# A recurrence's chunk matrices: 128x128 products on block-diagonal tiles, or 64x64 blocks on quarters of the array

## The chip, the cores and the metric

The kernel runs on one core of a Trainium2 chip. The metric is the device time of one execution in microseconds, median of several runs. Engines: TensorE (PE in the profile, its weight loads PEld), VectorE (DVE), ScalarE (ACT), GpSimd (POOL, unused) and SyncE (SP), whose queue issues all DMAs.

## The reference, cut to what matters

Two transformer blocks in fp32 over 1024 tokens with 1024 channels. The first (latent attention, Fourier mixing, SwiGLU) is not touched. The second adds banded attention and a recurrence ("RWKV-7 time mix"), gates and merges them, and ends in a feed-forward part. The recurrence is over 8 heads of 64 channels; per token and head it updates a 64x64 state:

```
p = p + (prev - p) * shift_mu ; r, k, v, cw, ca, cg = split(p)
decay = exp(-exp(-softplus(-(w0 + tanh(cw) @ w2)) - 0.5)) ; a = sigmoid(a0 + ca @ a2) ; g = sigmoid(cg) @ g2
kk = normalised(k * k_k) ; k = k * (1 + (a - 1) * k_a)
step:  sa = state @ (-kk) ; state = state * decay + outer(sa, kk * a) + outer(v, k) ; y = state @ r
y = group_norm(y) * ln_w + ln_b + sum(r * k * r_k) * v ; y = y * g
```

The kernel does not step token by token. Within a chunk of 64 tokens it forms the matrices of the decayed products of a, b = kk * a, k and r with one another, inverts I minus the strictly triangular one, and gets from it, for each chunk, a 64x64 map of the state (MT), an addition (NN), a map to the output (R2) and an output from zero (Y0). Only "state = MT * state + NN" is serial over chunks.

## The kernel before, in words

Every engine runs one long program (class Program); engines meet by semaphores whose numbers come from a first, counting pass (`wait_ge` on a named event). A PSUM bank is claimed with `k.bank(group)`, which turns through the banks, and the claim waits for the reader of the last tenant.

The recurrence is in class Mixer. It is cut into 8 units j: head pair hp = j // 2 (two heads, one in partitions 0 to 63 and one in 64 to 127) and half th = j % 2 of the tokens (512 tokens, 8 chunks). While unit j's matrices are made, unit j+1 "enters" (its a, b, k, r are shifted, decayed and turned to rows) and unit j-1 "leaves" (eight serial state steps, the output product yt, group normalisation, gate). The three are Python generators on each engine; `together` takes one round of each in turn until all have ended, and that is the whole order of work:

```
together(*[self.chunk_tensor(e, j, s) for s in range(2)], *behind, *ahead)
```

So in each round the matrices of head s = 0 stand first, then those of s = 1, then the leaving unit's work, then the entering unit's. PE, ACT and DVE have such a line each (from L3386 on).

Matrices (`chunk_tensor`, `chunk_scalar`, `chunk_vector`, L3001 to L3238): a tile M of 128x(4x128) holds four pairs of chunks of one head; each 128x128 block is block-diagonal in its two 64-token chunks, cut so by a mask. The pair products ("a", "n", "ak", "arb", "ark") contract 64 channels of one head into 128x128. Fifteen kinds of 128x128 products follow in each strand s: squarings of the 16-block-diagonal part (a2, n2, a4, n4, a8), the inverse of that part (x2, x4, x8), and a substitution in four steps for the rest (y0, r1, y1, r2, y2, r3, y3). ACT copies the plain results out of PSUM (L3120), DVE masks (L3175) or adds (L3180). At the end r2m and y0m write R2 and Y0 into 64 partitions each, and mt0, nn0, mt1, nn1 are 64x64x64 products, four or eight in a row on one quarter of PE's array.

Entering (`enter_*`, L2831 to L2989): decay and rate (L199 from TH, WA), the sums over a head (from CN "bones"), four turns by PE (L2868) and their copies by ACT (L2874), and elementwise work on 128x512 halves H. ACT's function changes five times a unit, each with a table load (L2885, L2898, L2900, L3296, L3298). Leaving (`leave_*`, L3251 to L3338): state products and adds (L3316), yt, sums for mean and variance, Ln and Exp for the root, gate. Behind the stage, the last unit leaves beside the first products of class Gates.

Of the kernel before, what the change touches and what calls it, by code (L numbers as in the profile page):

```python
# [34 lines left out]
def shape_constants():  # L35
# [50 lines left out]
class Quiet:  # L86
# [7 lines left out]
    reciprocal = memset = tensor_tensor_scan = dma_start = skip  # L94
# [2590 lines left out]
class Mixer:  # L2685
# [9 lines left out]
    def __init__(self, k, into):  # L2695
# [24 lines left out]
        self.Rt, self.At, self.Bt, self.Kt, self.Atm, self.Btm, self.Ktm, self.Vtm = [tile(o) for o in (124, 128, 132, 136, 88, 92, 96, 100)]  # L2720
        self.GN = [half(148), half(150)]
        self.SCM = half(120)
        mats = [k.sb("M", [128, 4, 128], 156 + 2 * i) for i in range(24)]
        self.mats = [self.strand(mats[0:12]), self.strand(mats[12:24])]
# [6 lines left out]
    @staticmethod  # L2731
    def strand(m):

        A16, N16, R1, R2m, Ak, Arb, Ark, A2, N2, Xm, RHS, Rv = m
        return A16, N16, R1, R2m, Ak, Arb, Ark, A2, N2, Xm, RHS, N2, Rv, A2
# [43 lines left out]
    def shifted(self, e, n, mu, dst, a, b, event, last):  # L2779

        raw, k = self.RAW[n % 3], self.k
        e.wait_ge(("fetched", n))
        if a == 0:
            e.op.tensor_tensor(dst[:, 1:b], raw[:, 0:b - 1], raw[:, 1:b], ALU.subtract).then_inc(*e.event("mix_dve", ("step", *event)))
            e.op.tensor_scalar(dst[:, 0:1], raw[:, 0:1], -1.0, None, ALU.mult).then_inc(*e.event("mix_dve", ("step_0", *event)))
            e.wait_ge(("step_0", *event))
        else:
            e.op.tensor_tensor(dst[:, 0:b - a], raw[:, a - 1:b - 1], raw[:, a:b], ALU.subtract).then_inc(*e.event("mix_dve", ("step", *event)))
            e.wait_ge(("step", *event))
# [3 lines left out]
    def sums_tensor(self, e, group, src, *ready, lo=0, hi=8):  # L2793

        bank, free = self.k.bank(group, lo, hi)
# [3 lines left out]
    def begin_tensor(self, e, lo, hi):  # L2799
        yield  # L2800
        yield
        yield from self.enter_tensor(e, 0, lo, hi)
# [22 lines left out]
    def chunk(self, j, what):  # L2825

        return [("mm", ("chunk", j, s, what)) for s in range(2)] if j >= 0 else []

    def enter_tensor(self, e, j, lo=0, hi=8):  # L2831
        k, hp = self.k, j // 2
        r, k_, v, ld, a_, L, kk, E1, E2, Q1 = self.T
        for part, what in ((0, "decay"), (64, "rate")):
            group = (what, j)
            bank, free = k.bank(group, lo, hi)
            e.wait_ge(free, "w2", "a2", "tanh", ("shifted", "hidden"))
            mm(e, k.out(group), self.WA[part:part + 64, hp * 128:(hp + 1) * 128], self.TH[part:part + 64, self.columns_of(j)], True, True).then_inc(
                *e.event("mix_mm", ("mm", group)))
        yield  # L2840
        yield
        yield
        self.sums_tensor(e, ("squares", j), Q1[:, :], ("kk_square", j), lo=lo, hi=hi)
        for _ in range(5):
            yield
        self.sums_tensor(e, ("bonus", j), E2[:, :], ("rk", j), lo=lo, hi=hi)
        yield
        yield
        self.rows_tensor(e, j, "v_rows", v, ("shifted", "v", j), lo, hi)
        yield  # L2850
        yield
        yield
        self.rows_tensor(e, j, "a_rows", self.At[:, self.columns_of(j)], ("at", j), lo, hi)
        for _ in range(5):
            yield
        self.rows_tensor(e, j, "b_rows", a_, ("b_end", j), lo, hi)
        yield
        self.rows_tensor(e, j, "k_rows", k_, ("k_end", j), lo, hi)
        yield
        yield  # L2860

    def rows_tensor(self, e, j, what, src, ready, lo, hi):

        group = (what, j)
        bank, free = self.k.bank(group, lo, hi)
        e.wait_ge(free, ready)
        for i in range(4):
            x = e.op.transpose(self.k.out(group, 128, 128 * i), src[:, i * 128:(i + 1) * 128], self.k.cst("ident"))  # L2868
        x.then_inc(*e.event("mix_mm", ("mm", group)))

    def rows_copy(self, e, j, what, dst):

        e.wait_ge(("mm", (what, j)), *self.chunk(j - 2, "nn1"), *self.rhs_read(j - 2))
        e.op.activation(dst[:, self.columns_of(j)], self.k.out((what, j)), ACT.Copy).then_inc(*e.event("mix_act", ("read", (what, j))))  # L2874

    def rhs_read(self, j):
        return [("rhs", "chunk", j, s, "rhs") for s in range(2)] if j >= 0 else []

    def enter_scalar(self, e, j):
# [4 lines left out]
        e.wait_ge(("mm", ("decay", j)), ("at", j - 1) if j else None)  # L2884
# [3 lines left out]
        e.wait_ge(("read", ("decay", j)))  # L2888
        e.op.activation(ld[:, :], ld[:, :], ACT.Copy, scale=-float(np.exp(-0.5))).then_inc(*done("log_decay"))
# [5 lines left out]
        for _ in range(5):  # L2895
            yield
        e.wait_ge(("read", ("squares", j)))
        e.op.activation(E1[:, :], E1[:, :], ACT.Ln, scale=float(2.0 ** 30)).then_inc(*done("kk_log"))  # L2898
        e.wait_ge(("kk_log", j))
# [3 lines left out]
        e.op.activation(Q1[:, :], L[:, :], ACT.Exp).then_inc(*done("decay_in"))  # L2903
        yield
        e.wait_ge(("log_before", j))
        e.op.activation(ld[:, :], ld[:, :], ACT.Exp).then_inc(*done("decay_before"))
# [4 lines left out]
        e.wait_ge(("mm", ("bonus", j)), ("read", ("bonus", j)))  # L2911
        e.op.activation(E2[:, :], L[:, :], ACT.Exp, scale=-1.0).then_inc(*done("decay_out"))
        yield
        e.wait_ge(("log_end", j))
        e.op.activation(E1[:, :], E1[:, :], ACT.Exp).then_inc(*done("decay_end"))
        yield
        self.rows_copy(e, j, "a_rows", self.Atm)
        for _ in range(5):
            yield
# [5 lines left out]
    def enter_vector(self, e, j):  # L2925
        k, hp, sl = self.k, j // 2, self.columns_of(j)
# [3 lines left out]
        a, b, last = sl.start, sl.stop, j % 2 == 1  # L2930
        e.wait_ge(("mm", ("k_rows", j - 1)) if j else None)
        self.shifted(e, 2 + 3 * hp, 4 + hp, k_, a, b, ("k", j), last)
        yield
        self.shifted(e, 3 + 3 * hp, hp, r, a, b, ("r", j), last)
        yield
        e.wait_ge(("mm", ("v_rows", j - 1)) if j else None)
        self.shifted(e, 4 + 3 * hp, 8 + hp, v, a, b, ("v", j), last)
# [4 lines left out]
        e.wait_ge(("rate_k", j), ("kk", j), ("shifted", "k", j))  # L2942
        e.op.scalar_tensor_tensor(k_[:, :], E2[:, :], 1.0, k_[:, :], ALU.add, ALU.mult).then_inc(*done("key"))
        yield
        e.wait_ge("scan", ("log_decay", j))
        e.op.tensor_tensor_scan(L[:, :], self.SCM[:, :], ld[:, :], 0.0, ALU.mult, ALU.add).then_inc(*done("sum_log"))
# [3 lines left out]
        yield  # L2950
        e.wait_ge(("key", j), ("shifted", "r", j))
        e.op.scalar_tensor_tensor(E2[:, :], r[:, :], k.vec("r_k", hp), k_[:, :], ALU.mult, ALU.mult).then_inc(*done("rk"))
        yield
        e.wait_ge(("sum_log", j))
        e.op.tensor_tensor(ld[:, :], L[:, :], ld[:, :], ALU.subtract).then_inc(*done("log_before"))
        yield
        e.wait_ge(("kk_rnorm", j))
        e.op.tensor_tensor(kk[:, :], kk[:, :], E1[:, :], ALU.mult).then_inc(*done("kk_unit"))
        yield
        e.wait_ge(("mm", ("bonus", j)), ("shifted", "v", j))  # L2960
        e.op.tensor_tensor(BV, k.out(("bonus", j)), v[:, :], ALU.mult).then_inc(*e.event("mix_dve", ("read", ("bonus", j))))
        yield
        L3 = L[:, :].rearrange("p (c s) -> p c s", s=64)
        E3 = E1[:, :].rearrange("p (c s) -> p c s", s=64)
        e.wait_ge(("kk_unit", j))
        e.op.tensor_tensor(E3, L3[:, :, 63:64].broadcast_to([128, 8, 64]), L3, ALU.subtract).then_inc(*done("log_end"))
        yield
        e.wait_ge(("decay_before", j), ("kk_unit", j), *self.chunk(j - 2, "ark"))
        e.op.scalar_tensor_tensor(self.At[:, sl], kk[:, :], -1.0, ld[:, :], ALU.mult, ALU.mult).then_inc(*done("at"))
        yield  # L2970
        e.wait_ge(("decay_in", j))
        e.op.tensor_copy(self.GC[:, a // 64:b // 64], Q1[:, 63:512:64]).then_inc(*done("gc"))
        e.op.tensor_tensor(self.Rt[:, sl], r[:, :], Q1[:, :], ALU.mult).then_inc(*done("rt"))
        yield
# [4 lines left out]
        yield  # L2979
        e.op.tensor_tensor(self.Kt[:, sl], k_[:, :], E2[:, :], ALU.mult).then_inc(*done("kt"))  # L2980
        yield
        e.wait_ge(("decay_end", j))
        e.op.tensor_tensor(a_[:, :], a_[:, :], E1[:, :], ALU.mult).then_inc(*done("b_end"))
        yield
        e.op.tensor_tensor(k_[:, :], k_[:, :], E1[:, :], ALU.mult).then_inc(*done("k_end"))
        yield
# [800 lines left out]
```

## Time and profile before

| | us |
|---|---|
| timed runs, median (3 runs, 3459.4 to 3460.91) | 3460.9 |
| the profiled execution's own time, as its page gives it: the span | 3467.7 |
| PE busy in the span | 3300.9 (95%) |
| DVE busy | 2089.3 (60%) |
| ACT busy | 1468.8 (42%) |
| recurrence, first to last matrix product | 2034 to 2571 |

"Busy" is the union of an engine's instructions. Matmuls overlap, so a group's mean duration is longer than the step from one to the next. The granted clock is a share of 2.4 GHz: 0.50 is 1.2 GHz. An fp32 matmul stands in the trace as two records (a transposing one as one).

### The profile page before, as it was taken

To read this page: it belongs to the slowest core of one execution; us is meant where nothing else is said; L and a number is where in the kernel's file an instruction comes from. 1 tells how busy PE (TensorE), PEld (TensorE's weight loads), DVE (VectorE), ACT (ScalarE), POOL (GpSimd) and SP (SyncE) were. 2 spreads that over 40 slices of the span, in tenths; PEclk is the share of its full clock that TensorE was granted. 3 is DMA by queue.
4 is the path that set the end of the run, shared out by engine and by line. 5 is a ranking of instruction groups with operands and counts; after the bars stand their busy time and mean duration, and the time that the engine had idled before them with its cause. 6 is when DMAs were issued, how large, how long until landed. Compare 5 with 4: busy or idle time off the path is not lost.

```text
span 3467.7 us, 42391 instructions
## 1 busy us (share of the span) xinstructions
PE 3300.9 (95%) x16430; PEld 2572.9 (74%) x16430; DVE 2089.3 (60%) x3506; ACT 1468.8 (42%) x2635; POOL 0.2 (0%) x4
## 2 busy tenths in 40 slices
PE   8989999999999999999999998898999999999888
PEld 7456666788888877788886677787874788777766
DVE  3535766567666567755555766655544466655665
ACT  2213555553333345533335544444421464554333
POOL 0000000000000000000000000000000000000000
PEclk9999999999999999999997999999999999999999
DMA  6510000232333465433333000000022524455645
GB/s 258 182 43 1 1 1 13 73 104 82 94 114 105 149 215 177 151 110 103 116 100 134 16 19 7 13 26 1 1 82 89 187 95 136 143 175 188 207 159 181
DMA packets 254505, 351.21 MB, mean 101 GB/s; under 512 B 12385, under 2 KB 142049, under 8 KB 251105
## 3 DMA queue, kind: packets, MB, share of 16 engines
q1 hardware_dynamic: 254304, 348.50, 29.9%
q8 instruction: 131, 2.15, 0.3%
q14 instruction: 70, 0.57, 0.1%
HBM read 264.04 MB, written 84.41 MB: 100 GB/s over the span
## 4 chain that ended last, share of the span: by engine, by line
PE 74%; DVE 11%; DMA 8%; issue 3%; ACT 3%; SPq 0%; DVEq 0%; ACTq 0%
PE ps L199 72%; DMA wr<-in_w_down 6%; DVE wl L407 2%; DVE M L3175 1%; DMA hid<-ob 1%; PE ps L1573 1%; DVE NM L2430 1%; PE ps L935 1%; ACT wh L383 1%; DVE Yf L508 0%; DVE ob L1326 0%; DVE QT L2449 0%; DVE RT L2448 0%; DVE QT L2451 0%; PE ps L2868 0%
## 5 line engine op out<-in xcount | busy, mean ns | idle before, releaser
L199 PE MATMUL ps<-ffn_h,wh 128*128 128x512 f32 x2176 | 673.1, 390 | 9.8 <-DVE ob L1326 6.5
L407 DVE TENSOR_TENSOR wl<-wr,wh 128x512 fp32r<-128x512 f32 x610 | 403.1, 687 | 278.4 <-ACT wh L383 275.7
L383 ACT ACTIVATE wh<-wr 128x512 fp32r<-128x512 f32 x610 | 364.5, 625 | 457.3 <-PE ps L199 265.0
L199 PEld LDWEIGHTS ps<-ffn_h,wh 128*128 128x128 f32 x2176 | 408.2, 188 | 99.8 <-DVE ob L1326 10.8
L199 PE MATMUL ps<-ffn_h,wl 128*128 128x512 f32 x1088 | 424.1, 390 | 0.0
L199 PE MATMUL ps<-in_h,wh 128*128 128x512 f32 x1200 | 371.0, 390 | 4.5 <-DVE Yf L837 4.5
L199 PE MATMUL ps<-wh,wh 128*128 128x512 f32 x756 | 302.0, 399 | 40.4 <-DVE wl L407 40.0
L199 PE MATMUL ps<-M,M 128*128 128x128 f32 (+1 forms) x2176 | 293.7, 295 | 37.4 <-DVE ybT L3337 16.6
L199 PEld LDWEIGHTS ps<-M,M 128*128 128x128 f32 (+1 forms) x2176 | 274.5, 200 | 57.1 <-DVE ybT L3337 18.0
L199 PE MATMUL ps<-wl,wh 128*128 128x512 f32 x756 | 299.6, 396 | 0.0
L199 PE MATMUL ps<-wh,wl 128*128 128x512 f32 x756 | 299.3, 396 | 0.0
L199 PEld LDWEIGHTS ps<-in_h,wh 128*128 128x128 f32 x1200 | 225.9, 188 | 52.2 <-DVE Yf L837 4.9
L199 PEld LDWEIGHTS ps<-ffn_h,wl 128*128 128x128 f32 x1088 | 204.5, 188 | 42.4
L199 PE MATMUL ps<-in_h,wl 128*128 128x512 f32 x600 | 234.2, 390 | 0.0
L199 PEld LDWEIGHTS ps<-wh,wh 128*128 128x128 f32 x756 | 145.2, 192 | 80.7 <-DVE wl L407 51.0
L3120 ACT ACTIVATE M<-ps 128x512 f32<-128x512 f32 x144 | 85.0, 596 | 208.6 <-PE ps L199 208.6
L199 PEld LDWEIGHTS ps<-wh,wl 128*128 128x128 f32 x756 | 145.2, 192 | 31.0
L199 PEld LDWEIGHTS ps<-wl,wh 128*128 128x128 f32 x756 | 145.0, 192 | 29.8
L407 DVE TENSOR_TENSOR wl<-s,wh 128x512 fp32r<-128x512 f32 x100 | 68.9, 689 | 121.0 <-ACT wh L383 121.0
L383 ACT ACTIVATE wh<-T 128x512 fp32r<-128x512 f32 x108 | 65.7, 629 | 153.8 <-DVE T L415 110.1
L199 PEld LDWEIGHTS ps<-in_h,wl 128*128 128x128 f32 x600 | 112.9, 188 | 23.5
L2326 ACT ACTIVATE E<-ps 128x512 f32<-128x512 f32 x160 | 95.0, 594 | 69.5 <-PE ps L199 66.4
(360 smaller groups left out, 5375.5 us busy)
## 6 DMA issues: line engine op xcount, KB each, us to landing
hid<-ob SPq DMA_DIRECT2D x174, 256.0 KB, 2.3
wr<-hid SPq DMA_DIRECT2D x84, 512.0 KB, 4.4
wr<-in_w_down SPq DMA_DIRECT2D x72, 512.0 KB, 3.6
wr<-in_w_up SPq DMA_DIRECT2D x54, 512.0 KB, 4.5
wr<-in_w_in SPq DMA_DIRECT2D x42, 512.0 KB, 5.2
kept<-ob SPq DMA_DIRECT2D x84, 256.0 KB, 2.0
late<-in_w_ada SPq DMA_DIRECT2D x16, 1024.0 KB, 7.4
wr<-in_w_out SPq DMA_DIRECT2D x32, 512.0 KB, 4.3
```

The lines of the kernel that those rows point to most:

```text
L199: return e.op.matmul(out, left, right, start=start, stop=stop, skip_group_check=True)
L383: e.op.activation(self.rows(s)[0], src, ACT.Copy).then_inc(*e.event(self.name + "_act", ("w_high", self.name, s)))
L407: e.op.tensor_tensor(lo, src, hi.bitcast(F32), ALU.subtract).then_inc(*e.event(self.name + "_dve", ("w_low", self.name, s), *done))
L935: x = e.op.transpose(k.out(group, 128, 128 * j), self.XN[:, t, c * 128:(c + 1) * 128], k.cst("ident"))
L1573: x = e.op.transpose(self.k.ps[:, self.turn_bank(i, c) * 512 + j * 128:self.turn_bank(i, c) * 512 + (j + 1) * 128], self.P[i % 2][:, (c + ...
L2326: e.op.activation(x, self.bank(n % 3), ACT.Exp).then_inc(*e.event("att_exp", ("exp", n)))
L2430: e.op.tensor_reduce(self.NM[:, h % 2, t, i:i + 1], self.bank(self.MAX + self.chunks.index(chunk) % 2, b - a), AX.X, ALU.max, negate=True) ...
L3120: e.op.activation(dst[:, :, :], self.four(name(what)), ACT.Copy).then_inc(*e.event("chunk_act", ("read", name(what))))
L3175: x = e.op.tensor_tensor(dst[:, :, :], self.four(name(what)), bc(m), ALU.mult)
```

## The change

Every block of a chunk becomes a 64x64 matrix, stored with the two chunks of a pair in the two partition halves (M is now 128x(4x64)); products run on quarters of the array, the two chunks (c) on the two diagonal quarters in turn, or, where head and chunk both choose the quarter, on all four in turn. Masks are 64 wide. "n" and "arb" share a product (nr, 128 columns: Bt with At and Rt side by side), "ak" and "ark" too (kr). The inverse's last part is changed: gt = Aoff' X and g = X' Aoff, g2 = g squared, and two additions y1, y2 in place of the four-step substitution. Both heads are in one generator, one after the other in each round, and 20 rounds stand for some 28. Banks are fixed. Some entering work goes: the exponents "log_before" and "log_end" with their Exp on ACT, and the scaling of the log decay; a and r share a tile AR, b_end and k_end are made from Bt and Kt. The order within a round is turned round.

```
-            together(*[self.chunk_tensor(e, j, s) for s in range(2)], *behind, *ahead)
+            together(*behind, *ahead, self.chunk_tensor(e, j))
...
+    BANK = {"a": 0, "nr": 2, "kr": 4, "a2": 2, "n2": 0, "a4": 2, "xn4": 0, "x4": 4, "a8": 2, "akv": 0, "x8": 4, "gt": 2, "g": 0, "y0": 4,
+            "g2": 2, "y1": 0, "y2": 4, "out": 2, "state": 4}
...
+        four_ways = [(u, s, c) for u in range(4) for s, c in ((0, 0), (1, 1), (0, 1), (1, 0))]
...
+        def pairs(what, left, right, n):
+            for s in range(2):
+                claim(s, what)
+            for u, s, c in four_ways:
+                x = mm(e, k.out(name(s, what), n, n * u, part(c)), left(s, u, c), right(s, u, c), True, True)
...
+        def prod(what, left, right, n, *ready):
+            for s in range(2):
+                claim(s, what, *[(r, name(s, r[1])) if isinstance(r, str) else (r[0], name(s, r[1])) for r in ready])
+                for u in range(4):
+                    for c in range(2):
+                        x = mm(e, k.out(name(s, what), n, n * u, part(c)), left(s)[part(c), u, :], right(s)[part(c), u, :], True, True)
+                done(x, s, what)
...
+        pairs("a", at, bt, 64)
+        pairs("nr", bt, ar, 128)
+        pairs("kr", kt, ar, 128)
+        prod("a2", of(N16), of(A), 64, ("a16", "a"), ("read", "nr"))
+        prod("n2", of(A), of(N16), 64)
+        prod("a4", of(N2), of(A2), 64, ("read", "n2"), ("read", "a2"))
+        prod("xn4", of(A2), of(XN), 128, ("x1", "nr"))
+        prod("x4", of(A), of(X), 64, ("read", "a4"), ("x2", "xn4"))
+        prod("a8", of(N4), of(A), 64, ("read", "xn4"))
+        prod("akv", of(Ak), of(values), 64, ("read", "kr"))
+        prod("x8", of(A2), of(X), 64, ("read", "a8"), ("read", "x4"))
+        prod("gt", of(Aoff), of(X), 64, ("read", "x8"), ("read", "a"))
+        prod("g", of(X), of(Aoff), 64)
+        prod("y0", of(X), of(AV), 128, ("read", "akv"))
+        prod("g2", of(G), of(GT), 64, ("read", "g"), ("read", "gt"))
+        prod("y1", of(GT), of(WU), 128, ("read", "y0"))
+        prod("y2", of(A2), of(WU), 128, ("read", "g2"), ("read", "y1"))
```

Each `pairs` or `prod` call of that list is a round of its own (a yield stands behind each, and an empty round ahead of gt), counted from 0; "out" and "state" are rounds 18 and 19, with 48 products of 64x64x64 each that visit the four quarters in turn. In `enter_*` all groups but the rate use bank 6:

```
-        self.rows_tensor(e, j, "a_rows", self.At[:, self.columns_of(j)], ("at", j), lo, hi)
+        self.rows_tensor(e, j, "a_rows", lambda i: self.AR[:, 0, c + 2 * i:c + 2 * i + 2, :].rearrange("p a n -> p (a n)"), ("at", j))
...
+        _, free = self.k.settle(group, 6)
...
-        e.op.activation(ld[:, :], ld[:, :], ACT.Copy, scale=-float(np.exp(-0.5))).then_inc(*done("log_decay"))
...
-        e.op.activation(ld[:, :], ld[:, :], ACT.Exp).then_inc(*done("decay_before"))
-        e.op.activation(E1[:, :], E1[:, :], ACT.Exp).then_inc(*done("decay_end"))
+        e.op.activation(E2[:, :], L[:, :], ACT.Exp, scale=self.RATE).then_inc(*done("decay_out"))
```

Rounds of note: on PE squares 5, bonus 10, v_rows 13, a_rows 15; the state steps 2 to 9 (two empty rounds are put ahead of them), yt 10, mean 11, var 13, gate 16, all in bank 7. On ACT, Ln and Exp of the entering unit 8 and 9, of the leaving one both in 14, the copy of v_rows in 14, behind them the copies of y0. On DVE the scan with the key in 8. The first gate products turn through banks 0 to 6.

## Rows read from the trace of the kernel before

**Rows 1.** Table by stretch: length, busy us (instructions) per engine, clock, DMA share, GB/s.
```profile
2034.00:2571.00 537.00, 482.43 (x4470) 435.57 (x4468) 322.28 (x594) 227.71 (x359) 0.00 (x0) 0.94 0.03 11
```

**Rows 2.** Chain of waits over 2034 to 2571, shares by line.
```profile
by line: PE ps L199 68.5%; DVE M L3175 9.1%; issue 2.3%; ACT L3296 1.7%; ACT L3298 1.7%; DVE H L2790 1.5%; ACT M L3120 1.4%; PE ps L2868 1.3%; DVE M L3180 1.1%; DVE ybT L3337 0.9%; ACT H L3296 0.9%; ACT H L3298 0.8%; DVE H L2788 0.8%; DVE H
```

**Rows 3.** PE's waits there: total us, times, longest.
```profile
PE ps L199 <- DVE ybT L3337: 16.6, 7, 2.6
PE ps L199 <- DVE STt L3316: 14.3, 17, 1.5
```

**Rows 4.** PE in time (start, us, instruction): gate products, first and last state steps.
```profile
2088.55 0.33 PE L199 MATMUL ps<-STt,F 64*64 64x64 f32 x4
...
2126.41 1.02 PE L199 MATMUL ps<-SG,WG 128*128 128x512 f32 x2
...
2480.74 1.02 PE L199 MATMUL ps<-SG,WG 128*128 128x512 f32 x2
...
2514.08 0.33 PE L199 MATMUL ps<-STt,F 64*64 64x64 f32 x4
...
2572.08 0.33 PE L199 MATMUL ps<-STt,F 64*64 64x64 f32 x4 [0.67 <-ACT F L3162]
```

**Rows 5.** PE in time: starts of runs of products of each form.
```profile
2052.16 1.95 PE L199 MATMUL ps<-M,M 128*128 128x128 f32 x16
2054.04 1.71 PE L199 MATMUL ps<-F,F 64*128 64x128 f32 x16
2055.68 0.66 PE L2868 MATMUL ps<-CN,H 128*128 128x128 f32 x4
...
2112.28 1.15 PE L199 MATMUL ps<-F,STt 64*64 64x64 f32 x32
2113.35 1.12 PE L199 MATMUL ps<-H,CN 128*128 128x512 f32 x2
...
2293.42 0.27 PE L199 MATMUL ps<-M,F 128*64 128x128 f32 x1
...
2296.41 0.79 PE L199 MATMUL ps<-F,M 64*64 64x64 f32 x13
...
2302.54 0.33 PE L199 MATMUL ps<-STt,F 64*64 64x64 f32 x4
```

**Rows 6.** Groups of PE instructions in 2034 to 2571: the largest.
```profile
L199 PE MATMUL ps<-M,M 128*128 128x128 f32 x1920 | 261.6, 297 | 37.4 <-DVE ybT L3337 16.6 <-DVE H L2949 12.3 <-ACT M L3120 6.8
```

**Rows 7.** Groups of ACT and DVE instructions in the same stretch: busy us, mean ns.
```profile
L3120 ACT ACTIVATE M<-ps 128x512 f32<-128x512 f32 x144 | 85.0, 596 | 208.6 <-PE ps L199 208.6
L3162 ACT ACTIVATE F<-ps 64x256 f32<-64x256 f32 x31 | 11.7, 378 | 21.7 <-PE ps L199 21.7
L3298 ACT ACT_TABLE_LOAD x7 | 9.0, 1283 | 0.1
L3296 ACT ACTIVATE H<-ps,CN 128x512 f32<-128x512 f32 x7 | 4.8, 689 | 0.1
L3298 ACT ACTIVATE H<-H 128x512 f32<-128x512 f32 x7 | 4.4, 631 | 0.1
...
L3180 DVE TENSOR_TENSOR M<-ps,M 128x512 f32<-128x512 f32 x96 | 66.2, 691 | 96.6 <-PE ps L199 96.0
L3234 DVE TENSOR_TENSOR F<-F,ps 64x256 f32<-64x256 f32 x32 | 13.4, 419 | 21.1 <-PE ps L199 19.5
```

**Rows 8.** Clock: short stretches (columns as rows 1), PE after a wait, the page's strip.
```profile
2106.00:2110.00 4.00, 4.00 (x21) 3.66 (x21) 1.09 (x2) 2.40 (x3) 0.00 (x0) 0.50 0.00 0
1870.00:1885.00 15.00, 15.00 (x44) 9.23 (x44) 7.85 (x16) 5.91 (x12) 0.00 (x0) 0.50 0.01 2
2082.00:2086.00 4.00, 4.00 (x86) 3.83 (x86) 2.43 (x6) 1.35 (x3) 0.00 (x0) 1.00 0.02 4
...
2105.78 3.78 PE L199 MATMUL ps<-M,M 128*128 128x128 f32 x16 [1.92 <-DVE H L2949]
...
PEclk9999999999999999999997999999999999999999
```

More of the change, by code:

```diff
@@ L3107, in halves @@
[L3107 to L3127 removed]
+        e.wait_ge(("bt", j), ("gc", j))
@@ new lines, in chunk_scalar, with keep @@
+    def chunk_scalar(self, e, j):
+        k, th = self.k, j % 2
+        A, Aoff, A2, N4, GT, G, NR, KR, XN, WU = zip(*self.mats)
+        name = lambda s, what: ("chunk", j, s, what)
+        def keep(what, dst, a=0, b=64, n=64, after=None):
+            for s in range(2):
+                e.wait_ge(("mm", name(s, what)), (after, name(s, what)) if after else None)
+                e.op.activation(dst(s), self.four(name(s, what), a, b, n), ACT.Copy).then_inc(*e.event("chunk_act", ("read", name(s, what))))
+        for _ in range(3):
+            yield
+        keep("a2", lambda s: A2[s][:, :, :])
+        yield
+        keep("n2", lambda s: XN[s][:, :, 64:128])
+        yield
+        keep("a4", lambda s: A[s][:, :, :])
+        yield
+        keep("xn4", lambda s: N4[s][:, :, :], 64, 128, 128, "x2")
+        yield
+        yield
+        keep("a8", lambda s: A2[s][:, :, :])
+        yield
+        keep("akv", lambda s: self.AV[:, 4 * th:4 * th + 4, s, 64:128])
@@ L3156, in chunk_scalar @@
-        e.op.activation(self.Y0[rows, c0:c0 + 512], k.out(name("y0m"), 512, 0, rows), ACT.Copy).then_inc(*e.event("chunk_act", ("read", name("y0m"))))
-        yield
-        for h in range(2):
-            yield
-            e.wait_ge(("mm", name(f"nn{h}")), *self.left(j - 2))
-            o = k.out(name(f"nn{h}"), 256, 0, rows).rearrange("p (u n) -> p u n", u=4)
-            e.op.activation(self.halves(self.NN, s, th, h), o, ACT.Copy).then_inc(*e.event("chunk_act", ("read", name(f"nn{h}"))))
-            yield
@@ L3253, in leave_tensor @@
         Yt, yc = self.GN
-        made = [("read", ("chunk", j, s, w)) for s in range(2) for w in ("nn1", "mt1", "r2m", "y0m")]
+        made = [("read", ("chunk", j, c, w)) for c in range(2) for w in ("out", "state")]
+        yield
+        yield
         for i in range(8):
@@ L3395, in scalar @@
             ahead = [self.enter_scalar(e, j + 1)] if j + 1 < self.UNITS else []
-            together(*[self.chunk_scalar(e, j, s) for s in range(2)], *behind, *ahead)
+            together(*behind, *ahead, self.chunk_scalar(e, j))
         e.mark(("end", "chunks", e.name))
@@ L3412, in vector @@
             ahead = [self.enter_vector(e, j + 1)] if j + 1 < self.UNITS else []
-            together(*[self.chunk_vector(e, j, s) for s in range(2)], *behind, *ahead)
+            together(*behind, *ahead, self.chunk_vector(e, j))
         e.mark(("end", "chunks", e.name))
```

562 lines of the change are left out of this document (259 added, 303 removed).

## The prediction, made before the changed kernel ran

> **What bounds the kernel now.** I read the page first, where TensorE (PE) stands far ahead of the other engines in busy time, so a gain must come out of PE's own stream or out of its waits. The table by stage then places the change: the recurrence lasts from 2034 to 2571 us, 537 us, with PE busy for 482.4 of them, DVE for 322.3 and ACT for 227.7, at a mean granted clock of 0.94 [rows 1]. The chain of waits over that stretch runs through PE for over two thirds [rows 2]. So the stage is bound by PE's queue, with 537.0 - 482.4 = 54.6 us in which PE waits, 6.8 us a unit over eight units; the list of waits names the two largest: for the departing unit's last product, and for the state's serial steps [rows 3]. ACT's and DVE's waits are for PE and cost nothing.
>
> A unit's length is read from its gate product, which comes once a unit: from 2126.41 to 2480.74 there are five periods, so 354.33 / 5 = 70.9 us. The first unit, with nothing departing, takes from about 2034 to 2088.6 (55 us), the last, with nothing entering, from 2514.1 to 2572.1 (58 us) [rows 4].
>
> **Each product of now.** The trace writes an fp32 product as two records, so 16 records are 8 products. What counts is start to start, not the mean duration, since matmuls overlap. From [rows 5]: eight 128x128 products 2054.04 - 2052.16 = 1.88 us, 0.235 each; eight with 64 rows 2055.68 - 2054.04 = 1.64, 0.205 each; the 24 products of r2m and y0m, alternating between two column halves, 2296.41 - 2293.42 = 2.99, so 0.0623 a record; the 48 quarter products of mt and nn, run four or more on one quarter before the next, 2302.54 - 2296.41 = 6.13, so 0.064 a record; and the departing unit's yt, 16 quarter products that alternate between the two diagonal quarters, 2113.35 - 2112.28 = 1.07, so 0.0334 a record. That last pair of numbers is the heart of the case: the same 64x64x64 product costs 0.128 us when its neighbour sits on the same quarter and 0.067 when it sits on the other diagonal one.
>
> **PE, what goes.** Per unit the two strands issue 120 full products (15 kinds x 4 x 2; the stage's 1920 records / 2 / 8 agree [rows 6]): 28.2 us; 40 pair products: 8.2; 8 of akv, full weights and half the columns, at most the full product's 0.235: 1.9; r2m and y0m 3.0; mt and nn 6.1. Sum 47.4 us.
>
> **PE, what comes.** Products on 64x64 blocks: "a" 16, ten products of width 64 (a2, n2, a4, x4, a8, akv, x8, gt, g, g2) 160, out 48, state 48: 272 of width 64. Width 128: nr, kr, xn4, y0, y1, y2: 96. The 160 have exactly yt's form and order: 0.0334. For "a", out and state, which visit all four quarters, nothing in the trace shows four at once: between 0.0167 (twice yt's overlap) and 0.064 (none); I take yt's row, the nearest. 544 records x 0.0334 = 18.2 us. Width 128 on quarters is not in the trace either: below, 0.0334 (if issue and not columns set yt's pace); above, 0.1025, the 64-row product's step with no overlap; I take 0.0623, the two-half row, which streams the same 128 columns in pairs. 192 x 0.0623 = 12.0. Sum 30.2 us, so PE loses 17.2 us of work a unit.
>
> Weighed against this stands a rule. The row shows yt's two quarters, which differ in array rows and write one PSUM bank at different partitions, running at 0.0334 [rows 5]. The Trainium skill, page "TensorEngine Tiling (Array Packing)", section "Gotcha 1: PSUM Pressure", says that different row tiles cannot access the same PSUM bank at the same time. By that rule alone the products on the diagonal (all but "a", nr, kr, out, state) would run one by one; by the row they overlap. The trace disagrees with it for width 64, so I follow the trace and keep the rule as a rival.
>
> **PE, what stays.** Decay and rate, two sums, four turns, eight states, yt, mean, var, gate: about 10.4 us a unit by like rows (the period's remainder after 47.4 of matrices, 6.8 of waits and 4.0 for the half clock, below, is 12.7 and holds it).
>
> **Waits.** In the new order each round issues departing, then entering, then matrix work, on every engine, and a matrix step is one round for both heads. A 256-element copy by ACT takes 0.378 us where the 512-element one took 0.596, and DVE's add 0.419 for 0.691 [rows 7]. ACT's chunk work falls from 18 + 2 copies of 0.59 and 4 of 0.378 (13.4 us) to 22 of 0.378 and 2 of 0.596 (9.5); three entering activations of about 0.6 go too. DVE's falls from about 25.5 us (28 operations of 0.69, the rest halves) to 18 x 0.42 + 8 x 0.69 = 13.1, and two entering subtractions of 0.68 go. With 227.7 / 8 = 28.5 and 322.3 / 8 = 40.3 us busy before [rows 1] ACT is left at 23, DVE at 27: neither can be the bound. What is late next is a queue: in round 14 ACT stands through the departing Ln and Exp, each with a table load of 1.283 [rows 7], and the copy of the entering values' turn before it copies y0: 1.28 + 0.69 + 1.28 + 0.63 + 0.60 = 4.5 us. Behind PE's y0 (32 x 0.0623 = 2.0 us) stands the turn of a_rows, which now shares bank 6 with v_rows and waits for that copy, and behind it g2 and everything of the matrices. With ACT 0.7 late from g, PE waits 4.5 + 0.7 - 2.0 = 3.2 us. Round 9 waits for the state add behind DVE's scan and key, and bonus behind rk: 1.8. Elsewhere the first head's reader (0.38 to 0.42) is covered by the second head's product (0.53). Together 5.0 a unit, estimated; bounds 0, and 13 if each of the 20 rounds adds 0.4 of unhidden handing over (a quarter-product group of 0.53 us is shorter than product, reader and two hand-overs together).
>
> **The clock.** After a wait PE runs at half: in 2106 to 2110 the granted clock is 0.50 (1.2 GHz), and 16 records take 3.78 us instead of 1.95 [rows 8, 5]. At 0.94 mean, 2 x 0.06 x 537 = 64 us of the stage stood at 1.2 GHz, costing half, 32 us or 4.0 a unit. Waits a unit shrink only from 6.8 to 5.0, so I keep 4.0 of loss.
>
> **Sum.** New period 30.2 + 10.4 + 5.0 + 4.0 = 49.6 us instead of 70.9: 21.3 x 6 units = 128. The first unit loses 17.2 (it had nothing departing to wait for), the last 17.2 and some 3 of rounds (20 instead of 28): 38 together. 166 us in all. The attention ahead gets the first entering unit in fewer rounds on two banks, hidden beside PE's full queue; the gate stage behind gets seven banks for eight: 0. The profiled execution has a span of 3467.7, 6.8 above the median of the runs (3460.9, 0.2%): 3467.7 - 166 = 3301.7 on its own scale, 3295 on that of the timed runs.
>
> **Rivals.**
> (1) More overlap: four quarters at once in "a", nr, kr, out, state halves 7.5 + 4.0 us, and shorter waits leave the clock at 2.4 GHz: 5.7 + 4.0 a unit, 78 in all: 3217. For it: DVE and ACT have room. Against: the half clock came after waits under 3 us, which remain. 0.12.
> (2) Rounds bind: handing over costs 13 and not 5 a unit, since a round now holds one matrix step and no other strand fills it: 8 x 8 = 64 more: 3359. For it: the single strand. 0.12.
> (3) The diagonal quarters do not overlap in one bank: 320 records go from 0.0334 to 0.064 and 128 from 0.0623 to 0.1025, 14.9 a unit, 119: 3414. Against it yt's row. 0.07. If no quarters overlap at all (the change does not do what it says), matrices take 544 x 0.064 + 192 x 0.1025 = 54.5 us, 7 more than now, and with the waits the period is 73.9: about 3485. 0.03.
> (4) The other side: the stage falls to 1.2 GHz and stays there. In 1870 to 1885, among the attention's small products, PE is busy all the time and the clock is 0.50 [rows 8]. If quarter products can't lift the clock once a wait has lowered it, PE's 40.6 us become 81.2, the period 86, 15 longer than now: 8 x 15 = 120 slower, 3580. It decides where 70.9 - 45.6 = 25.3 of the 40.6 us, 62% of PE's work, runs at half clock. Against it: six microseconds of quarter products (2082 to 2088) (four of them in the row) ran at 1.00 [rows 8], and each fall in the stage ended within some 7 us. 0.05.
> The Trainium skill, page "TensorE: Matmul & The Clock Gate", section "What's actually happening", makes throttled the default and says that activity releases it; the attention's stretch shows that a busy engine alone need not, the recurrence that it mostly does.
>
> **Chances and range.** The forecast has 0.61, own range 3255 to 3335 (waits 0 to 10). The attention's half-clock stretch can also end earlier or later with the entering work's new order: the page's clock strip has 0.7 to 0.8 in that slice of 86.7 us [rows 8], so 35 to 52 us at 1.2 GHz, which cost 17 to 26: as much faster, or about as much slower; this is inside the range. From (1) to (2) 0.85 is held, less tails: 3215 to 3380. Faster by over 0.2% (7 us, about what a measurement here can tell from no change): forecast, (1), (2), (3)'s first half, 0.92; within 0.2% 0.01 (the edge of (3)'s second half); slower 0.07.
>
> **What would show it.** Right: the gate product returns every 45 to 54 us; the 64-wide products stand at 0.03 us a record in alternating quarters, the 128-wide at 0.053 to 0.063; PE's largest wait is ahead of the a_rows turn, for ACT; DVE and ACT at some 27 and 23 us a unit. Wrong: 0.06 a record for the diagonal products (3); a granted clock near 0.5 through the stage (4); PE waits over 10 us a unit spread over all rounds (2).

## The result, and the profile after

| us | before | changed |
|---|---|---|
| timed, median | 3460.9 (3459.4 to 3463.49) | 3264.78 (3259.7 to 3271.17, 4 runs) |
| profiled span | 3467.7 | 3257.9 |
| PE busy | 3300.9 | 3078.1 |
| recurrence, first entering product to the first product of the gate stage behind it (yaT,PW) | 2033.8 to 2572.3 | 2020.2 to 2355.7 |

The changed kernel takes 0.943 of the time before (95% interval 0.9417 to 0.9447). Some executions of either kernel run 100 to 120 us longer at a lower mean clock; the comparisons leave them out.

The stage itself shrank by 203.0 us, it began 13.6 us earlier, and what follows it took 6.8 us more. Together that is 209.8, the difference of the two spans. In the table by stretch (columns as in [rows 1]), the changed stage, and 45 us in its middle:

```profile
2022.00:2352.00 330.00, 275.22 (x6415) 218.56 (x6411) 212.97 (x454) 176.90 (x335) 0.00 (x0) 0.97 0.06 19
2118.00:2163.00 45.00, 37.29 (x852) 28.90 (x846) 29.30 (x65) 24.67 (x46) 0.00 (x0) 0.96 0.04 14
```

Beside [rows 1] the stage is still PE's (83% busy), but PE idles as much as it did, 54.8 us against 54.6, in a stage 203 us shorter. The chain of waits over 2022 to 2352, by line, answers to [rows 2]; PE's share fell from 68.5 to 54%:

```profile
by line: PE ps L198 54.0%; issue 4.7%; PE ps L2868 4.4%; DVE MM L3187 3.8%; ACT L3303 2.7%; ACT L3305 2.7%; DVE MM L3180 2.7%; DVE H L2798 2.6%; DVE H L2963 2.4%; ACT F L2883 1.8%; DVE STt L3325 1.6%; DVE F L2976 1.5%; DVE H L3332 1.5%; ACT
```

PE's waits in it (total us, times, longest). The two of [rows 3] are gone or small, and a new one is largest, six times 3.2 us: the turn of a_rows (L2868) waits for ACT's copy of v_rows (L2883).

```profile
PE ps L2868 <- ACT F L2883: 19.0, 6, 3.2
PE ps L198 <- DVE MM L3187: 7.5, 9, 0.9
PE ps L198 <- ACT F L2883: 7.2, 6, 1.2
PE ps L198 <- DVE STt L3325: 5.9, 19, 0.5
PE ps L198 <- issue: 4.3, 8, 1.2
```

ScalarE's own rows at that wait show what stands ahead of the copy: Ln (L3303) and Exp (L3305) of the departing unit, each with its table load.

```profile
2080.98 1.28 ACT L3303 ACT_TABLE_LOAD   x1
...
2082.98 1.28 ACT L3305 ACT_TABLE_LOAD   x1
...
2084.81 0.58 ACT L2883 ACTIVATE F<-ps 128x512 f32<-128x512 f32 x1
```

PE in time, one unit from its first entering product (TH,WA) to the next's, and the last such product but one, which gives the period (start, us, instruction; the answer to [rows 4, 5]):

```profile
2056.39 1.13 PE L198 MATMUL ps<-TH,WA 64*128 64x512 f32 x4 [1.17 <-ACT F L2883]
2057.44 0.69 PE L198 MATMUL ps<-F,AR 64*64 64x64 f32 x32
2057.96 1.06 PE L198 MATMUL ps<-AR,F 64*64 64x128 f32 x32
2058.96 0.27 PE L198 MATMUL ps<-STt,F 64*64 64x64 f32 x2
...
2065.88 1.92 PE L198 MATMUL ps<-MM,M 64*64 64x128 f32 x32
2067.62 0.28 PE L198 MATMUL ps<-STt,F 64*64 64x64 f32 x4
...
2078.80 0.66 PE L2868 MATMUL ps<-CN,H 128*128 128x128 f32 x4
2079.38 1.15 PE L198 MATMUL ps<-M,MM 64*64 64x64 f32 x32
2080.37 1.92 PE L198 MATMUL ps<-AV,MM 64*64 64x128 f32 x32
2085.44 1.10 PE L2868 MATMUL ps<-CN,AR 128*128 128x128 f32 x4 [3.16 <-ACT F L2883]
2086.48 1.97 PE L198 MATMUL ps<-M,M 64*64 64x64 f32 x32
2088.38 1.37 PE L198 MATMUL ps<-SG,WG 128*128 128x512 f32 x2
2089.68 4.04 PE L198 MATMUL ps<-MM,M 64*64 64x128 f32 x64
2094.59 0.46 PE L198 MATMUL ps<-MM,MM 64*64 64x64 f32 x16 [0.88 <-DVE MM L3187]
...
2096.15 0.66 PE L2868 MATMUL ps<-CN,H 128*128 128x128 f32 x4
2096.74 0.34 PE L198 MATMUL ps<-F,MM 64*64 64x64 f32 x8
...
2098.68 0.66 PE L2868 MATMUL ps<-CN,H 128*128 128x128 f32 x4
2100.56 1.13 PE L198 MATMUL ps<-TH,WA 64*128 64x512 f32 x4 [1.22 <-ACT F L2883]
...
2278.14 1.13 PE L198 MATMUL ps<-TH,WA 64*128 64x512 f32 x4 [1.20 <-ACT F L2883]
```

Period: (2278.14 - 2056.39) / 5 = 44.35 us, forecast 49.6, before 70.9. Steps from start to start: "a" 2057.96 - 2057.44 = 0.52 us for 32 records in all four quarters, 0.0163 each; nr 1.00 for 32 of width 128, 0.031; a diagonal product of width 64 2080.37 - 2079.38 = 0.99, 0.031; of width 128 2067.62 - 2065.88 = 1.74, 0.054; out 2096.15 - 2094.59 = 1.56 for 96, 0.0163; state 2098.68 - 2096.74 = 1.94 for 96, 0.020. Behind the 3.16-us wait the turn takes 1.10 us where its like took 0.66, and M,M 1.97 where it took 1.15: half clock. The table by stretch agrees, before and behind the wait:

```profile
2060.00:2085.00 25.00, 20.39 (x430) 15.87 (x424) 19.49 (x47) 16.06 (x30) 0.00 (x0) 1.00 0.01 2
2085.30:2088.60 3.30, 3.16 (x37) 2.71 (x38) 0.93 (x2) 1.55 (x5) 0.00 (x0) 0.53 0.02 5
```

From the turn to the products behind the gate product it is 2089.68 - 2085.44 = 4.24 us; at full clock 0.58 + 0.98 + 1.02 = 2.6: 1.7 us lost, once a unit.

Groups of ACT and DVE in the stage (busy, mean ns), against [rows 7]: the readers have the sizes that the other shapes of before gave.

```profile
L3132 ACT ACTIVATE M<-ps 128x256 f32<-128x256 f32 x112 | 41.1, 381 | 67.8 <-PE ps L198 54.7 <-DVE MM L3187 10.8
L3187 DVE TENSOR_TENSOR MM<-ps,MM 128x256 f32<-128x256 f32 x48 | 19.2, 422 | 16.6 <-PE ps L198 16.5
```

### The profile page after: what moved, and what is told of

The parts are those of the page before. It is cut to its first block, busy times and chain, and to the rows that moved or that the text cites. A ratio compares the mean times of both kernels' runs of the same rounds, so it can differ in the third digit from the quotient of the medians.

```text
span 3257.9 us, 46321 instructions
## 1 busy us (share of the span) xinstructions
PE 3078.1 (94%) x18478; PEld 2345.0 (72%) x18478; DVE 1979.6 (61%) x3370; ACT 1417.1 (43%) x2611; POOL 0.2 (0%) x4
## 4 chain that ended last, share of the span: by engine, by line
PE 73%; DVE 11%; DMA 8%; issue 4%; ACT 3%; SPq 0%; DVEq 0%; ACTq 0%
PE ps L198 71%; DMA wr<-in_w_down 6%; DVE wl L406 3%; DMA hid<-ob 2%; PE ps L1572 1%; DVE NM L2429 1%; PE ps L934 1%; ACT wh L382 1%; PE ps L2868 0%; DMA wr<-hid 0%; DVE MM L3187 0%; DVE ob L1325 0%; DVE Yf L507 0%; DVE QT L2448 0%; DVE RT L2447 0%
## 5 line engine op out<-in xcount | busy, mean ns | idle before, releaser
L198 PE MATMUL ps<-ffn_h,wh 128*128 128x512 f32 x2176 | 672.9, 390 | 12.4 <-DVE ob L1325 9.2
L198 PEld LDWEIGHTS ps<-ffn_h,wh 128*128 128x128 f32 x2176 | 408.0, 188 | 101.7 <-DVE ob L1325 13.5
L198 PE MATMUL ps<-wh,wh 128*128 128x512 f32 x756 | 301.5, 399 | 46.1 <-DVE wl L406 46.0
L2429 DVE TENSOR_REDUCE NM<-ps 128x1 f32<-128x512 f32 (+1 forms) x192 | 105.9, 593 | 23.2 <-PE ps L198 22.6
L198 PE MATMUL ps<-hT,ring 128*128 128x512 f32 (+1 forms) x256 | 112.1, 594 | 0.0
L414 DVE TENSOR_TENSOR T<-wr,T 128x512 f32<-128x512 f32 x81 | 52.8, 689 | 91.6 <-DMA wr<-in_w_down 91.6
```

The lines of the kernel that those rows point to most:

```text
L198: return e.op.matmul(out, left, right, start=start, stop=stop, skip_group_check=True)
L414: e.op.tensor_tensor(out, left, right, op).then_inc(*e.event(self.name + "_dve", ("slot_sum", self.name, s), *done))
L2429: e.op.tensor_reduce(self.NM[:, h % 2, t, i:i + 1], self.bank(self.MAX + self.chunks.index(chunk) % 2, b - a), AX.X, ALU.max, negate=True) ...
```

## The experiments

Each kernel is the changed one with the edit shown, and its time is to be held against 3264.78 (above) and 3259.96 (c_changed_again, below) for the changed kernel itself. A "period" is the mean distance of the units' first entering products (TH,WA) in the middle of the stage, over four or five units. A "ratio" is the time over that of the kernel before, with its 95% interval.

**How much the quarters overlap.** The same products, in the order of one quarter after the other:

```
-        four_ways = [(u, s, c) for u in range(4) for s, c in ((0, 0), (1, 1), (0, 1), (1, 0))]
+        four_ways = [(u, s, c) for s, c in ((0, 0), (1, 1), (0, 1), (1, 0)) for u in range(4)]
-                for u in range(4):
-                    for c in range(2):
+                for c in range(2):
+                    for u in range(4):
```

In out and state too, the quarter is now the outer loop.

> The changed kernel with the same products on the same quarters, but all products of one quarter behind one another (four in a row in a product, twelve in out and state). Theory A (the gain is overlap of neighbours on different quarters): 64-wide records go back to 0.064 us and 128-wide to about 0.10, which adds 10.7 + 6.1 (diagonal products) + 1.5 + 4.5 (pairs) + 8.8 (out, state) = 31.6 us a unit, less some 3 that fall into the wait ahead of the a_rows turn: 200 to 250 us, so 3465 to 3515 us, the whole gain gone. Theory B (the gain comes from smaller copies, adds and fewer rounds, and the blocks' order is second): under 60 us more, below 3325 us.

Measured: 3374.91 and 3383.67 us, some 115 more than the changed kernel; period 57.9, 13.5 longer. The order alone is worth over half of the change's gain; the other 80 us (fewer and smaller products, smaller readers, fewer rounds, the clock) are not parted by any run. PE in time, the same places of one unit:

```profile
2217.22 1.54 PE L198 MATMUL ps<-MM,M 64*64 64x64 f32 x32
2218.68 1.12 PE L198 MATMUL ps<-H,CN 128*128 128x512 f32 x2
...
2241.74 0.41 PE L198 MATMUL ps<-MM,MM 64*64 64x64 f32 x4 [0.88 <-DVE MM L3183]
...
2246.91 0.66 PE L2868 MATMUL ps<-CN,H 128*128 128x128 f32 x4
```

Out takes 2246.91 - 2241.74 = 5.17 us for 96 records, 0.054, against 0.0163: with twelve products on a quarter there is nearly no overlap. But a diagonal step, four products on a quarter, takes 2218.68 - 2217.22 = 1.46, 0.046 a record. Its like in the changed kernel, also ahead of an H,CN product, takes 1.08, 0.034:

```profile
2073.82 1.15 PE L198 MATMUL ps<-MM,M 64*64 64x64 f32 x32
2074.90 1.13 PE L198 MATMUL ps<-H,CN 128*128 128x512 f32 x2
```

So the order sets the overlap, but theory A's 0.064 for runs of four was too high, and the cost came out at half of what it expected. Not all of the 115 us is pace: in e1's profile the mean clock of the stage is 0.93 against 0.97, some 65 us at 1.2 GHz against 20, which is about 22 us of loss; and PE's waits there shrank from 57 to 38 us.

Two quarters at a time instead of four, only in "a", nr, kr, out and state:

```
-        four_ways = [(u, s, c) for u in range(4) for s, c in ((0, 0), (1, 1), (0, 1), (1, 0))]
+        four_ways = [(u, s, c) for d in (0, 1) for u in range(4) for s, c in ((0, d), (1, 1 - d))]
```

and the same order in out and state.

> The changed kernel with a, nr, kr, out and state on only two quarters at a time (first (0,0) with (1,1), then (0,1) with (1,0)). Theory A (four quarters at once are worth what their steps say: 0.0163 instead of the forecast 0.0334 us a record): adds 0.5 + 1.0 + 1.0 + 1.5 + 1.3 = 5.3 us a unit, about 40 us, 3305 us. Theory B (these products stand beside waits of ACT and DVE, PE's steps there do not set the period): under 12 us more.

Measured: 3281.38 (3277.5 to 3284.49), ratio 0.9473 (0.9453 to 0.9494); period 47.7. Out in PE's rows:

```profile
2146.05 0.45 PE L198 MATMUL ps<-MM,MM 64*64 64x64 f32 x8 [0.88 <-DVE MM L3187]
...
2148.82 0.66 PE L2868 MATMUL ps<-CN,H 128*128 128x128 f32 x4
```

2.77 us for 96, 0.029 a record: in out my row from yt was right for two quarters, and four at once nearly halve it. The cost, 17 to 21 us, is about half of the 40 expected, because "a" (0.018 a record) and, partly, nr and kr lost less than half their pace. And some 8 of it are the clock's: about 37 us of this stage ran at 1.2 GHz against 20.

Which two quarters? e2 paired the diagonal ones. Here pairs on the same rows of the array, then pairs on the same columns:

```
-        four_ways = [(u, s, c) for u in range(4) for s, c in ((0, 0), (1, 1), (0, 1), (1, 0))]
+        four_ways = [(u, d, c) for d in (0, 1) for u in range(4) for c in (0, 1)]
```

```
-        four_ways = [(u, s, c) for u in range(4) for s, c in ((0, 0), (1, 1), (0, 1), (1, 0))]
+        four_ways = [(u, s, d) for d in (0, 1) for u in range(4) for s in (0, 1)]
```

with out and state in pairs ((0, d), (1, d)) in the first, and ((d, 0), (d, 1)) in the second.

> Neighbouring products run in two quarters that read the same rows of the array and write different halves of PSUM's partitions; the third and fourth quarter come only in the next eight. Compared with e2_two_quarters (3281 us, diagonal quarters, 0.029 us a record of width 64). Theory A (two quarters overlap whichever two they are, as long as they are not the same one): the four-ways steps have 0.029 to 0.032 us a record, and the time is 3275 to 3290 us. Theory B (quarters on the same rows share what feeds the rows, and run one behind the other): 0.055 to 0.064 us a record in the four-ways steps, 352 records a unit, +9 to +12 us a unit against e2, about 3360 us.

> As e10_same_rows, but neighbouring products share the columns of the array, so that they write the same partitions, in two banks where the bank differs by chunk half, and read different rows. Theory A (any two different quarters overlap): 0.029 to 0.032 us a record of the four-ways steps, 3275 to 3290 us. Theory B (quarters on the same columns run one behind the other): 0.055 to 0.064 us a record, about 3360 us. If e10 and e11 come out apart, rows and columns are not alike, and the kernel's order (all four in turn) owes its 0.0163 us to the one that overlaps.

Measured: 3274.97 (one execution) and 3279.15 (3278.68 to 3279.62), periods 47.0 and 46.1; "a" took 0.59 us in both, 0.018 a record. Out of e10, then of e11:

```profile
2145.70 0.45 PE L198 MATMUL ps<-MM,MM 64*64 64x64 f32 x8 [0.88 <-DVE MM L3187]
...
2148.39 0.43 PE L198 MATMUL ps<-MM,F 64*64 64x64 f32 x4
2148.76 1.11 PE L2868 MATMUL ps<-CN,H 128*128 128x128 f32 x4
```

```profile
2148.43 0.45 PE L198 MATMUL ps<-MM,MM 64*64 64x64 f32 x8 [0.87 <-DVE MM L3187]
...
2151.20 0.66 PE L2868 MATMUL ps<-CN,H 128*128 128x128 f32 x4
```

3.06 us (its last quarter already at half clock) and 2.77. Theory A holds for out: which two quarters they are does not matter, the pace is 0.029 with two and 0.0163 with four. In "a" two quarters reach 0.018, for which the runs show no cause. The pairs on the same columns wrote to two banks in out; with both in one bank they were not tried. Nor were four quarters in one bank: in "a", nr, kr, out and state the quarters that share a bank read the same rows. Only the diagonal products have different rows in one bank.

**The order of departing, entering and matrix work.**

```
-            together(*behind, *ahead, self.chunk_tensor(e, j))
+            together(self.chunk_tensor(e, j), *behind, *ahead)
```

and the same for ScalarE's and VectorE's lists.

> The changed kernel with the old order in a round: matrices, then departing, then entering work, on all three engines. Theory A (the order is second to the quarter products): within 15 us of 3265 us; the wait of the a_rows turn for the copy of v_rows stays, since both are entering work. Theory B (putting departing and entering work ahead is a main part of the gain, since the matrices then wait behind fewer foreign instructions when their operands are late): at least 5 us a unit lost, 3305 us or more.

Measured: 3276.3 (3274.85 to 3277.88), ratio 0.9459 (0.9441 to 0.9478), 11.5 to 16 us more; period about 45.9. PE's waits in 2060 to 2320, where the changed kernel has 19.0 us in six:

```profile
PE ps L2868 <- ACT F L2883: 28.2, 11, 4.2
```

The new order shortens this wait, but is a small part of the gain beside the tiles. Its worth is partly the clock's, whose mean in the stage is 0.93 here and 0.97 in the changed kernel. The kernel before with the new order alone was not tried.

**The entering work off the path.** Three of ScalarE's entering operations and two of VectorE's, which the change removed, are put back with their results unused:

```
+        if j:
+            e.op.activation(self.D[1][:, :], L[:, :], ACT.Exp, scale=-self.RATE).then_inc(*done("decay_before"))
...
```

> The changed kernel with the entering work that it dropped put back as idle copies into scratch, units 1 to 7: three activations of 128x512 on ACT (rounds 1, 10, 12) and two subtractions on DVE (rounds 9, 12); their results are not used. Theory A (ACT and DVE have room, that work is off the path): 0 to 8 us more than 3265. Theory B (the two queues are the path once PE is short): 3 x 0.55 + 2 x 0.6 = 2.9 us a unit, 20 us more.

Measured: 3257.72, 3262.17, 3277.83; ratio 0.9429 (0.9391 to 0.9468); period 44.4, as without the edit: it is off the path.

**The copies' slack.** Each of ScalarE's copies of products is made twice:

```
+                e.wait_ge(self.spare[0])
+                o = self.D[4][:, 0:4 * (b - a)].rearrange("p (u n) -> p u n", u=4)
+                e.op.activation(o, self.four(name(s, what), a, b, n), ACT.Copy).then_inc(...)
                 e.op.activation(dst(s), self.four(name(s, what), a, b, n), ACT.Copy)...
```

> Each of ScalarE's 18 copies of a unit's products out of PSUM is made twice, the first time into a buffer that nobody reads, so every operand that a copy delivers comes one copy (0.38 to 0.63 us) later: the result is the reference's. Theory A (TensorE's own records bind a round: in the changed kernel's steady stretch it is busy 37.3 of 45 us, and none of its waits of over 1 us a unit is for such a copy): copies have slack, the period of 44.4 us grows by under 2 us, and the time is 3265 to 3278 us. Theory B (rivals' rounds bound: each round lasts as long as product, copy, next product): nine rounds of a unit become 0.4 to 0.9 us longer, the period rises by 4 to 8 us, and the time is 3290 to 3325 us, with new waits of TensorE for L3132's copies.

Measured: 3267.35 (3266.56 to 3268.33), ratio 0.943 (0.9415 to 0.9445); period 45.1, 0.7 more. Theory A. PE's waits in 2045 to 2345 (the changed kernel has 19.0 in the first):

```profile
PE ps L2869 <- ACT F L2884: 21.2, 6, 3.5
...
PE ps L198 <- ACT MM L3137: 0.3, 1, 0.3
```

The copies' own line appears with 0.3 us. The hand-overs by way of ScalarE's copies have slack; VectorE's were not delayed by any run.

**The wait for v_rows' copy.** Ln and Exp of the departing unit, each with a table load, stand ahead of that copy in ACT's queue. Here they come two rounds later, and the operations behind them too:

```
-        yield
-        yield
+        for _ in range(4 if j < self.UNITS - 1 else 2):
+            yield
         e.wait_ge(("mm", ("var", j)))
```

and likewise the gate product two rounds later, the normalising product and the affine step three.

> The changed kernel with the departing unit's Ln and Exp (two table loads, 3.9 us of ACT) moved from round 14 to round 16, behind the copies of v_rows, y0 and g2, and what hangs on them two to four rounds later (units 0 to 6). Theory A (that queue is what PE waits for ahead of the a_rows turn, and the wait is what lowers the clock once a unit): the wait of 3.2 us goes and with it the half-clock window's 1.7 us, less some 1 for y1's own wait: 3 to 4.5 us a unit, 20 to 30 us, 3235 to 3245 us. Theory B (the matrices' chain of hand-overs binds anyway, the wait moves to y1 or out): under 6 us.

Measured: 3233.24 (3228.91 to 3246.48), ratio 0.9334 (0.9304 to 0.9364), 27 to 32 us under the changed kernel. PE's waits in 2060 to 2320, and the stage in the table by stretch:

```profile
PE ps L198 <- ACT F L2883: 7.2, 6, 1.2
...
PE ps L2868 <- ACT F L2883: 0.4, 1, 0.4
```

```profile
2022.00:2322.00 300.00, 270.01 (x6454) 216.09 (x6456) 213.15 (x455) 179.07 (x335) 0.00 (x0) 0.99 0.07 20
```

The period is 39.4, 4.95 shorter, and the stage (first entering product to the gate stage) 302.7 us, 32.8 shorter. That is not 3.2 of wait and 1.7 of clock in each unit, as expected. PE's waits fell by some 25 us: 19 ahead of the a_rows turn, and some 6 ahead of out (DVE MM L3187, 7.5 us before, 1.4 now), where the gate product, now two rounds later, fills the gap. Stretches at half clock fell only from six to two, which gives some 7 us.

To part the wait from the clock, PE was given work in the place of the wait:

```
+        if j >= 2:
+            e.wait_ge(("read", ("chunk", j - 1, 0, "g")))
+            for _ in range(3):
+                mm(e, k.out(("chunk", j - 1, 0, "g")), k.cst("bones"), self.SG[:, 0:512], True, True)
```

> From the third unit on TensorE makes three 128x512 products that nobody reads in the place where it waits some 3 us for the copy ahead of the a rows; the result is unchanged. Theory A (it is the wait that lets the clock fall behind it): the stretches at half clock that stand once in each unit's recurrence go for five of the units, 1.7 us each, so -5 to -10 us: 3251 to 3258 us, or about 3260 if the filler delays the rows by what it saves. Theory B (the half clock comes from the small tiles' activity, not from the wait): the stretches stay, and the filler adds up to 1 us a unit where its end comes later than the copy: 3260 to 3272 us.

Measured: 3263.97, 3248.75, 3250.36; ratio 0.9392 (0.9371 to 0.9413). In the profiled execution (the first) the period is 42.4, 2.0 shorter, and the whole stage is at full clock:

```profile
2045.00:2361.00 316.00, 280.26 (x6361) 217.36 (x6357) 212.69 (x454) 176.51 (x335) 0.00 (x0) 1.00 0.06 19
```

```profile
2147.67 2.31 PE L198 MATMUL ps<-SG,CN 128*128 128x512 f32 x5
2150.37 0.66 PE L2872 MATMUL ps<-CN,AR 128*128 128x128 f32 x4 [0.39 <-ACT F L2887]
2150.96 1.15 PE L198 MATMUL ps<-M,M 64*64 64x64 f32 x32
```

The turn and M,M now take 0.66 and 1.15. So the small tiles alone do not bring the half clock; with the idle time filled it stays away. But idle time of this length does not bring it each time either. In e7_k_rows_bank (below), where the same wait stands, one unit went on at full clock:

```profile
2132.92 0.66 PE L2868 MATMUL ps<-CN,AR 128*128 128x128 f32 x4 [3.16 <-ACT F L2883]
2133.50 1.15 PE L198 MATMUL ps<-M,M 64*64 64x64 f32 x32
```

Three of the six such waits in e10_same_rows have no half clock behind them (mean clock 1.00 in 2091.5 to 2095, 2279.4 to 2283 and 2323.4 to 2327). That this one execution is no faster than the changed kernel comes from ahead of the stage, which it reached 22.8 us later; the stage itself was 12.2 us shorter.

**The wait for k_rows' bank** at each unit's first product (1.2 us, six times), with and without the later Ln and Exp:

```
-        self.rows_tensor(e, j, "k_rows", ..., ("k_end", j))
+        self.rows_tensor(e, j, "k_rows", ..., ("k_end", j), 2 if j else 6)
```

> The changed kernel with the last turn of the entering unit (k_rows) in bank 2 instead of bank 6, for units 1 to 7, so that the next unit's decay product in bank 6 need not wait for its copy. Theory A (the 1.2 us of wait at each unit's start is that bank): 6 x 1.2 = 7 us less. Theory B (the next product waits elsewhere: nr for the same copy): no change.

> Both edits of the two kernels beside it. Theory A: their sum, 27 to 37 us less, 3228 to 3240 us. Theory B: no more than the better one alone.

Measured for e7: 3252.85, 3258.67, 3260.56, ratio 0.9397 (0.9368 to 0.9426); the wait moves, to the rate's sigmoid one product on, and the time is not told apart from the changed kernel's, though the period is 43.35, 1.0 shorter:

```profile
PE ps L198 <- ACT H L2895: 7.1, 6, 1.2
```

e8_both: 3229.34 (3225.51 to 3245.14), ratio 0.9324 (0.9285 to 0.9364): the fastest version, not told apart from e6.

**The changed kernel again**, beside e6 to e8:

> The changed kernel itself, as the measure for the three beside it on the same chip: 3258 to 3272 us, period of a unit 44.4 us, 3.2 us of wait ahead of the a_rows turn in each of six units.

3259.96 (one execution); the same waits as above, period 44.2.

## Why the prediction was right, and where its terms were not

The time (3264.8) is in the range, 30 under the forecast of 3295. One of its signs was just missed: the units follow one another every 44.35 us, where it had 45 to 54. By its steps, per unit:

| us a unit | forecast | measured |
|---|---|---|
| matrix products | 30.2 | 22.8 |
| other products | 10.4 | 12.4 |
| waits | 5.0 | 7.4 |
| half clock | 4.0 | 1.7 |
| period | 49.6 | 44.35 |

Measured: the products are 0.52 ("a") + 2.0 (nr, kr) + 10 x 0.98 + 4 x 1.74 + 1.56 + 1.94 = 22.8; the waits 54.8 x 44.35 / 330 = 7.4; the clock from the steps above. Other products are what is left: by their own steps they come to some 11, and the rest is the ends of products ahead of waits.

- **PE binds the stage, its products set the gain: right.** e1 moves nothing but their order and costs 115 us; e5 and e9 load ACT, e5 also DVE, and cost next to nothing.
- **The diagonal products: right.** 0.031 against 0.0334 forecast; width 128 0.054 against 0.0623. The Trainium skill's rule ("TensorEngine Tiling (Array Packing)", "Gotcha 1: PSUM Pressure"), by which different row tiles could not use one bank at the same time, does not hold for this form in this kernel. A diagonal step takes 1.08 us in turn and 1.46 in e1, and without overlap the pace would be [rows 5]'s 0.064 a record.
- **The term that was mis-sized: the products in all four quarters.** For "a", out and state I took yt's 0.0334 and for nr and kr 0.0623; they ran at 0.0163, 0.0163, 0.020 and 0.031. 224 records cost 4.0 us instead of 7.5, nr and kr 2.0 instead of 4.0: 5.5 of the 7.4. This is rival 1's mechanism; e2 shows it apart, and e10 and e11 show that in out any two quarters reach only 0.029. Rival 1 priced it at 5.7 a unit, rightly, but its time of 3217 also took the half clock away, and that stayed until e6.
- **Waits: the place right, the sum low.** The wait ahead of the a_rows turn came out at 3.16 us for the 3.2 forecast, for the reason given, as ACT's rows and e6 show. I had not seen that the next unit's first product waits 1.2 us for k_rows' copy (it stood behind other matrix work before), nor 0.9 us ahead of out for DVE's wide add (0.69): there no departing or entering work is left to fill the round (in e6 the later gate product fills it).
- **Half clock: 1.7 instead of 4.0.** I carried the old loss over because the waits hardly shrank. In the changed kernel they are spread thinly, and only behind one of them a unit (3.2 us) does the clock fall. e12 shows that filling it is enough, e6 that removing it gains the wait itself as well. What decides whether the clock falls behind a given wait stays open (e7, e10).
- **Rounds (rival 2): wrong.** Its price was 13 us a unit, and all waits together are 7.4; e9 adds to the copies and costs 0.7. **No overlap (3), and a stage at 1.2 GHz (4): wrong**, the mean clock is 0.97.
- **Ahead of and behind the stage.** The attention's half-clock stretch was 47.8 us long in the profile before and 20.5 in the one after, and half of that difference, 13.6, is the earlier start. With the same code ahead of the stage it lasted 20.5 in nine of the thirteen profiles of changed kernels, 27.3 in two, 44.4 in e5's and 58.0 (in two pieces) in e12's. Its length differs between executions of the same code, so from one profile of the kernel before it can't be said that these 13.6 of the 209.8 us are the change's doing. What follows the stage took 902.2 us against 895.4, and 901 to 904 in every other profile of a changed kernel but e12's (895.9); why, stays open.

In sum, matrices -7.4, other +2.0, waits +2.4, clock -2.3: 5.3 a unit below the forecast, over six units 32 us. That this is close to the miss of 30 is in part luck. On the profile's own scale the miss is 44 us (3257.9 against 3301.7): 32 in the six units, 6 in the first and the last, which were put at 37.8 us each and took 36.2 and some 33, and 13.6 less 6.8 ahead of and behind the stage, which the forecast had put at nothing.

## What to carry to other kernels

Block-sparse 128x128 products are worth cutting into quarter tiles above all when neighbours in TensorE's queue sit on different quarters (in e1's order the changed kernel still gained some 80 us, with all its other edits): look at the order of issue before the count of products, and price four quarters at a quarter of the lone one, not at a half. When the stream shrinks, the queue of the engine that empties PSUM becomes the next limit: look for long operations (a table load between two functions) ahead of a short copy that TensorE needs. A wait costs more than its length if the clock falls behind it; here 3.2 us of waiting cost 4.9 where it fell, and 3.2 where it did not.

## What the runs showed of the hardware

- fp32 quarter products of width 64, per record: about 0.054 in runs of twelve on one quarter, 0.046 in runs of four products, 0.029 to 0.034 with two quarters in turn (in out: diagonal, same rows or same columns alike; but 0.018 in "a"), 0.0163 with four in "a" and out and 0.020 in state; a lone quarter of [rows 5] had 0.064.
- In one execution (e12_filler) TensorE was busy for 42.85 of 44.3 us in 1870.4 to 1914.7, all of it at half clock (0.50), and for 280.3 of 316 us in 2045 to 2361, all of it at full clock: a high busy share alone did not go with the full clock.
- In the changed kernel each of the six 3.2-us waits was followed by half clock, and none of the waits of up to 1.2 us; but e6_root_later, whose longest waits are 1.2 us, still had two such stretches. In e10_same_rows three of six 3.2-us waits had none, while 13.7 us at half clock began at 2148.1, where the wait ahead had been 0.88 us and had ended 2.4 us before.
